# Expert results of a mixture-of-experts layer: block stores with an indexed gather, against an indexed scatter with plain loads

## What is computed

```python
# t: (512, 1024) normalised tokens; 4 groups x 8 experts, hidden width 512
g_sel  = argmax(t @ w_group + b_group)               # one group per token
e_logit = (t @ w_er[g_sel] + b_er[g_sel])            # 8 experts of that group
top_v, top_i = top_k(e_logit, 2)                     # two experts per token
gate   = softmax(top_v) * p_group
y[tok] = sum over its 2 experts e of gate * ((silu(t @ w_gate[e]) * (t @ w_up[e])) @ w_down[e])
x = x + y
```

## Time and profile before

| | |
|---|---|
| median of 3 runs | 1780.88 us (1779.61 to 1782.25) |
| profiled execution | 1782.86 us, span 1780.8 us |
| TensorE (PE) busy | 1412.7 us, 79% |
| VectorE (DVE) | 543.8 us, 31% |
| ScalarE (ACT) | 247.5 us, 14% |
| GpSimd (POOL) | 173.4 us, 10% |
| granted TensorE clock, mean | 0.906 of full speed |
| DMA | 486.05 MB, mean 273 GB/s |

### The profile page before, as it was taken

The page is one execution under the profiler, slowest core; times in us unless marked ns, Lnnn a source line. Parts: engine busy times, 40 slices in busy tenths (PEclk is TensorE's granted clock), DMA queues, the critical chain, the costliest instruction groups (busy, mean ns, idle before and its releaser), DMA issues. The chain is left out here.

```text
span 1780.8 us, 18695 instructions
## 1 busy us (share of the span) xinstructions
PE 1412.7 (79%) x7013; PEld 687.5 (39%) x7013; DVE 543.8 (31%) x1125; ACT 247.5 (14%) x501; POOL 173.4 (10%) x215
## 2 busy tenths in 40 slices
PE   6998756986988787878858978795998788788782
PEld 3444745542333333333313466653333233333330
DVE  6998598223101110110123156424011011011014
ACT  2201312110000000000001035410110000000001
POOL 0007160001000000000020000000110000000002
PEclk9999977987999999998987989996999899899896
DMA  7511403337999999999984200405899999999994
GB/s 233 157 56 25 38 13 145 151 145 281 390 406 404 408 417 411 409 408 407 412 333 164 95 1 1 177 37 227 325 399 408 406 411 406 404 409 410 407 417 169
DMA packets 75027, 486.05 MB, mean 273 GB/s; under 512 B 16752, under 2 KB 23536, under 8 KB 50016
## 3 DMA queue, kind: packets, MB, share of 16 engines
q1 hardware_dynamic: 53984, 440.26, 62.7%
q0 software_dynamic: 9472, 23.94, 4.3%
q10 hardware_dynamic: 11520, 21.15, 3.2%
HBM read 465.91 MB, written 27.79 MB: 277 GB/s over the span
## 5 line engine op out<-in xcount | busy, mean ns | idle before, releaser
L588 PE MATMUL psum<-ring,work 128*64 128x512 f32 x992 | 491.9, 654 | 133.6 <-DMA ring<-in_moe_w_up 130.7
L589 PE MATMUL psum<-ring,work 128*64 128x512 f32 x992 | 492.9, 655 | 0.0
L588 PEld LDWEIGHTS psum<-ring,work 128*64 128x64 f32 x992 | 144.3, 150 | 452.9 <-issue 449.4
L601 PE MATMUL psum<-ring,work 128*64 128x512 f32 x992 | 226.5, 598 | 31.2 <-DVE work L739 31.2
L736 DVE TENSOR_TENSOR work<-work,psum 64x512 f32<-64x512 f32 x64 | 44.1, 690 | 641.6 <-ACT work L693 599.3
L693 ACT ACTIVATE work<-psum 64x512 f32<-64x512 f32 x64 | 37.8, 591 | 842.1 <-PE psum L589 842.1
L589 PEld LDWEIGHTS psum<-ring,work 128*64 128x64 f32 x992 | 144.2, 150 | 0.0
L601 PEld LDWEIGHTS psum<-ring,work 128*64 128x64 f32 x992 | 66.6, 136 | 145.0 <-issue 125.2
L742 DVE COPY work<-psum 128x512 f32<-128x512 f32 x64 | 44.2, 691 | 247.7 <-PE psum L601 247.7
L1527 PE MATMUL psum<-ring,hT 128*128 128x512 f32 x256 | 112.1, 600 | 2.1 <-ACT work L1646 2.1
L883 POOL COPY ints<-ints 64x1 uint32 (+1 forms) x64 | 11.4, 179 | 818.7 <-PE psum L580 774.1
(11 more groups left out here) (350 smaller groups left out, 1425.8 us busy)
## 6 DMA issues: line engine op xcount, KB each, us to landing
ring<-in_moe_w_gate SPq DMA_DIRECT2D x62, 2048.0 KB
ring<-in_moe_w_up SPq DMA_DIRECT2D x62, 2048.0 KB, 23.2
ring<-in_moe_w_down SPq DMA_DIRECT2D x62, 2048.0 KB, 23.8
y_dram<-work ACTq DMA_DIRECT2D x128, 128.0 KB
ring<-in_hyb_w_in SPq DMA_DIRECT2D x5, 2048.0 KB, 9.7
ring<-in_swa_w_qkv SPq DMA_DIRECT2D x3, 2048.0 KB, 15.8
y_dram<-ones POOLq DMA_DIRECT2D x1, 4096.0 KB, 19.9
ring<-in_hyb_w_out SPq DMA_DIRECT2D x2, 2048.0 KB, 7.8
```

What stands on the lines that cost most here:

```text
L588: nc.tensor.matmul(bank[2 + b][0:BLK, :], XT[b][:, c, :], g[:, c, :], start=c == 0, stop=c == KC - 1)
L589: i = nc.tensor.matmul(bank[2 + b][BLK:P, :], XT[b][:, c, :], u[:, c, :], start=c == 0, stop=c == KC - 1)
L601: i = nc.tensor.matmul(bank[6 + b][BLK * hf:BLK * (hf + 1), :], HTE[b][:, c, :], d[:, c, hf * HALF:(hf + 1) * HALF], start=c == 0, stop=c ...
```

## The change

`y_dram` now has two rows of 2 KB (left and right half) for each assignment: row 2 * (512 k + token) + half. The router makes a second list: the one-hot block table is multiplied by 2 * (512 k + token) - 8192 and TensorE multiplies it twice with the place table, into the two halves of 128 partitions; with 8192 + half added (`SCL`) that is the target row of each partition of `YE`, and 8192 or more in an empty place. GpSimd issues, for each block, one indexed DMA that writes the 128 half rows of `YE` to their targets and skips those over 2047. In its loop GpSimd gathers the tokens of block e + 4 and then scatters the results of block e. ScalarE issues no stores. When all scatters have landed, SyncE reads the overflow count and issues eight plain loads of 512 KB for the combine, whose semaphores are now one for each tile. The calculation of `ROWI` and the fill at the start go.

```diff
-        y_dram = dram("y_dram", [NBLK * BLK, D])
+        y_dram = dram("y_dram", [2 * 2 * S, HALF])
...
+    put("srow", 2 * (np.arange(2 * NT)[None, :] * P + p[:, None]) - 2 * NOROW)
+    put("half", p[:, None] // BLK)
...
+            bs = shp(BL2, 8, NBLK)
+            pe.wait_ge(g_S.s, l + 1)
+            for hf in range(2):
+                for a in range(8):
+                    i = nc.tensor.matmul(bank[5][BLK * hf:BLK * (hf + 1), 0:NBLK], pl[:, a, :], bs[:, a, :], start=a == 0,
+                                         stop=a == 7)
+            i.then_inc(g_Sm.s, 1)
...
-            V(tv.tensor_tensor(bl, ins_dim(rt("ob"), 2, NBLK), ins_dim(cst("eid")[:, 0:NBLK], 1, 8), ALU.is_equal))
+            V(tv.tensor_tensor(bs, ins_dim(rt("ob"), 2, NBLK), ins_dim(cst("eid")[:, 0:NBLK], 1, 8), ALU.is_equal))
...
+            V.sync()
+            V(tv.tensor_tensor(bs, bs, ins_dim(cst("srow"), 2, NBLK), ALU.mult), g_S)
...
-            pi, a, b = rt("q").bitcast(I32), rt("qp").bitcast(I32), rt("ei").bitcast(I32)
-            V(tv.tensor_copy(pi, rt("pos")))
...
-            V(tv.tensor_copy(ROWI, rt("row")))
...
+            dve.wait_ge(g_Sm.s, l + 1)
+            V(tv.tensor_scalar(SCL, bank[5][:, 0:NBLK], cst("half"), 2.0 * NOROW, ALU.add, ALU.add), g_sc)
...
-            def store(e, par):
-                act.wait_ge(e_y, b0 + e + 1)
-                store_y1(act, par, e, y_st[par])
...
-                    dve.wait_ge(y_st[1 - par], 16 * b0 + (e - 3 - (1 - par)) * 16 + 32)
+                    dve.wait_ge(y_st[1 - par], 8 * b0 + (e - 3 - (1 - par)) * 8 + 16)
...
+            for t in range(NT):
+                for k in range(2):
+                    r0 = 2 * (S * k + P * t)
+                    sp.dma_start(YK[NT * k + t], y_dram[r0:r0 + 2 * P, :].rearrange("(p h) d -> p (h d)", h=2)).then_inc(
+                        yk_ld[t], 16)
...
+            def scatter_y(b, done):
+
+                pool.indirect_dma_start(y_dram, bass.IndirectOffsetOnAxis(SSTG[b], 0), YE[b], None, bounds_check=4 * S - 1,
+                                        oob_is_err=False).then_inc(done, 16)
+
+            def store(e, par):
+                pool.wait_ge(e_y, b0 + e + 1)
+                col = SCL[:, e:e + 1] if isinstance(e, int) else SCL[:, bass.ds(e, 1)]
+                pool.tensor_copy(SSTG[par], col).then_inc(e_sst, 1)
+                pool.wait_ge(e_sst, b0 + e + 1)
+                pool.sem_inc(pool_passed, 1)
+                scatter_y(par, y_st[par])
+
             fetch(0, 0)
             fetch(1, 1)
-            with pool.Fori(0, (NE - 2) // 2) as i:
+            fetch(2, 0)
+            fetch(3, 1)
+            pool.wait_ge(g_sc.s, l + 1)
+            with pool.Fori(0, (NE - 4) // 2) as i:
                 for k in range(2):
-                    fetch(i * 2 + 2 + k, k)
+                    fetch(i * 2 + 4 + k, k)
+                    store(i * 2 + k, k)
+            for e in range(NE - 4, NE):
+                store(e, e % 2)
...
-            for i in (k * NT + t for t in range(NT) for k in range(2)):
-                pool.indirect_dma_start(YK[i], None, y_dram, bass.IndirectOffsetOnAxis(ROWI[:, i:i + 1], 0)).then_inc(yk_ld[i], 16)
...
             for t in range(NT):
+                dve.wait_ge(yk_ld[t], 32 * (l + 1))
                 for k in range(2):
                     i = k * NT + t
-                    dve.wait_ge(yk_ld[i], 16 * (l + 1))
...
-            pool.dma_start(y_dram[NE * BLK:].rearrange("(p r) (c d) -> p (r c) d", p=P, d=P), ins_dim(ONES[:, :], 1, n)).then_inc(
-                fill_st, 16)
-            pool.wait_ge(fill_st, 16)
```

More of the change, by code:

```diff
@@ L64 @@
                   ("before", P), ("eye16", GC), ("gtie", NGRP), ("etie", EPG), ("eid", BLK), ("bidx", MAXOV + 1),
-                  ("tok", NT), ("place", BLK)]:
+                  ("tok", NT), ("place", BLK), ("srow", 2 * NT), ("half", 1)]:
     _COLS[_name] = (_N, _N + _w)
@@ L192, in encoder @@
             "consts_loaded", "x_loaded", "gain_loaded", "s5_rows_loaded", "s5_c_loaded", "s5_b_loaded", "router_loaded"))
-        fill_st = sem("y_rows_filled")
         pe_passed, pool_passed, sp_passed = (sem(n) for n in ("pe_wait_passed", "pool_wait_passed", "sp_wait_passed"))
@@ L347, in encoder @@
         INTS = sb("ints", 64 + NBLK + 2, U32)
-        ROWI = INTS[:, 0:8]
         PL1, BL1 = cut(WK, 11776, 8 * BLK), cut(WK, 12288, 8 * NBLK)
@@ L353, in encoder @@
         STG = [INTS[0:BLK, 64 + NBLK + b:65 + NBLK + b] for b in range(2)]
+        BL2 = cut(WK, 12288 + 8 * NBLK, 8 * NBLK)
+        SCL = rt("big")[:, 0:NBLK].bitcast(U32)
+        SSTG = [INTS[:, b:b + 1] for b in range(2)]
         assert 20 + MAXOV + 2 <= 64
@@ L362, in encoder @@
         g_L, g_Lm, g_sl = Count("router_places"), Count("router_lists_mm"), Count("router_lists")
+        g_S, g_Sm, g_sc = Count("router_targets"), Count("router_targets_mm"), Count("router_target_lists")
+        e_sst = sem("blk_targets")
         xg_ld = [sem(f"x_block{b}") for b in range(2)]
@@ L368, in encoder @@
         y_st = [sem(f"y_stored{b}") for b in range(2)]
-        yk_ld = [sem(f"y_rows{i}") for i in range(8)]
+        yk_ld = [sem(f"y_rows{t}") for t in range(NT)]
         ov = [{k: sem(f"ov{l}_{k}") for k in ("w", "i", "xg", "xt", "xe", "gu", "a", "h", "ht", "he", "dn", "y", "st")}
@@ L529, in dve_router @@
             V.sync()
-            bl = shp(BL1, 8, NBLK)
+            bl, bs = shp(BL1, 8, NBLK), shp(BL2, 8, NBLK)
             V(tv.tensor_tensor(shp(PL1, 8, BLK), ins_dim(rt("pos"), 2, BLK), ins_dim(cst("place"), 1, 8), ALU.is_equal))
-            V(tv.tensor_tensor(bl, ins_dim(rt("ob"), 2, NBLK), ins_dim(cst("eid")[:, 0:NBLK], 1, 8), ALU.is_equal))
+            V(tv.tensor_tensor(bs, ins_dim(rt("ob"), 2, NBLK), ins_dim(cst("eid")[:, 0:NBLK], 1, 8), ALU.is_equal))
             V.sync()
             for k in range(2):
-                V(tv.tensor_tensor(bl[:, NT * k:NT * (k + 1)], bl[:, NT * k:NT * (k + 1)], ins_dim(cst("tok"), 2, NBLK),
+                V(tv.tensor_tensor(bl[:, NT * k:NT * (k + 1)], bs[:, NT * k:NT * (k + 1)], ins_dim(cst("tok"), 2, NBLK),
                                    ALU.mult), g_L if k else None)
+            V.sync()
+            V(tv.tensor_tensor(bs, bs, ins_dim(cst("srow"), 2, NBLK), ALU.mult), g_S)
             V(tv.tensor_tensor(rt("cle").rearrange("p (b e) -> p b e", e=NE), ins_dim(rt("inc"), 1, MAXOV + 1),
@@ L720, in act_moe @@
                     xe(i * 2 + 2 + k, k)
-                    store(i * 2 + k, k)
                     silu(i * 2 + 2 + k, k)
-            for b in range(2):
-                store(NE - 2 + b, b)
             def body(j):
@@ L851, in sp_moe @@
             for b in range(2):
-                sp.wait_ge(y_st[b], 16 * NE * (l + 1))
+                sp.wait_ge(y_st[b], 8 * NE * (l + 1))
             def body(j):
@@ L859, in body @@
                     load_block_w(sp, ex + NE * l, 1, k, o["w"])
-                sp.wait_ge(o["y"], j + 1)
-                store_y1(sp, 1, j + NE, o["st"])
-                sp.wait_ge(o["st"], j * 32 + 32)
+                sp.wait_ge(o["st"], j * 16 + 16)
                 sp.sem_inc(sp_passed, 1)
             overflow_blocks(sp, l, body)
[L867 to L871, removed]
+            for t in range(NT):
[3 more added lines that the diff above has]
+                        yk_ld[t], 16)
         def pool_moe(pool, l, Q):
@@ L908, in body @@
                 pool.tensor_copy(STG[1], SLL[:, bass.ds(j + NE, 1)]).then_inc(o["i"], 1)
-                pool.wait_ge(o["i"], j + 1)
+                pool.wait_ge(o["i"], j * 2 + 1)
                 pool.sem_inc(pool_passed, 1)
                 gather_x(1, o["xg"])
-                pool.wait_ge(o["xt"], j + 1)
-            overflow_blocks(pool, l, body)
-            for b in range(2):
-                pool.wait_ge(y_st[b], 16 * NE * (l + 1))
-            overflow_wait(pool, l, "st", 32)
-            for i in (k * NT + t for t in range(NT) for k in range(2)):
-                pool.indirect_dma_start(YK[i], None, y_dram, bass.IndirectOffsetOnAxis(ROWI[:, i:i + 1], 0)).then_inc(yk_ld[i], 16)
[L922 to L926, removed]
+                pool.wait_ge(o["y"], j + 1)
+                pool.tensor_copy(SSTG[1], SCL[:, bass.ds(j + NE, 1)]).then_inc(o["i"], 1)
+                pool.wait_ge(o["i"], j * 2 + 2)
+                pool.sem_inc(pool_passed, 1)
+                scatter_y(1, o["st"])
+                pool.wait_ge(o["st"], j * 16 + 16)
+                pool.sem_inc(pool_passed, 1)
+            overflow_blocks(pool, l, body)
         def dve_combine(dve, l, V):
             for t in range(NT):
+                dve.wait_ge(yk_ld[t], 32 * (l + 1))
                 for k in range(2):
                     i = k * NT + t
-                    dve.wait_ge(yk_ld[i], 16 * (l + 1))
                     V(nc.vector.scalar_tensor_tensor(xv[:, t, :], YK[i], gates[:, i:i + 1], xv[:, t, :], ALU.mult,
@@ L2065, in _ @@
             pool.wait_ge(z_mm.s, 1)
```

(4 more changed lines are left out.)

## The result

| | before | after |
|---|---|---|
| median | 1781.06 us (7 runs, 1776.51 to 1784.21) | 1768.62 us (7 runs, 1764.55 to 1773.32) |
| ratio to before, 95% interval | | 0.9927 [0.9908, 0.9946] |
| profiled execution | 1782.86 us, span 1780.8 | 1765.54 us, span 1763.7 |
| first to last silu of the 32 experts, layer 0 / layer 1 | 478.87 / 479.00 us | 471.53 / 472.43 us |
| DMA | 486.05 MB | 473.48 MB |

The change saves 12.4 us, 0.7%. The forecast was a saving of 42 us, and the range ended at 1767: the time lies just above it, nearest to the rival "only the bytes count" (1763).

What follows compares the result with a forecast made beforehand. DMA engines were taken to pace the expert stages. 1782.9 - 41.8 (scatters) + 1.4 (router) - 1.5 (clock) + 0 = 1741.0, with the median 2.0 below the profiled run: 1739 us, range 1713 to 1767.

Steps and rivals of the forecast that it cites:

- only the bytes count: Rival: a result scatter saves only 0.31 us for its halved bytes, 18 us over 58 stores, so 1763 us; chance 0.20.
- What bounds the kernel: Expert stages: they run at the pace of the DMA engines (share 1.01), with TensorE having some 4 us room an expert.
- The price of a store: Expert stages: a store pair costs 1.44 us, from the rate's fall after its issue (1.47) and the stage's mean (1.43).
- Whichever the cost goes with, it halves: Scatter for two stores: half the bytes, pieces and DMAs, so 0.72 us saved on each of 58 stores, -41.8 us.
- the lower bound that the prediction had: Price of one result scatter if its bytes alone count: 0.131 MB / 430 = 0.31 us.
- the token gathers on that queue show no such fall here: Expert stages: token gathers on the software queue leave the rate at 430 GB/s; argued against software-made descriptors slowing two engines.
- Router, TensorE: Router: 16 added products take 3.9 us and delay layer 0's transposes by 1.4 us; zero in layer 1.
- Clock: TensorE at expert 0: added products fill idle gaps, so the higher clock may come earlier; -1.5 us for both layers together.
- Issue on GpSimd, ends of the layers, fill: Moving issue from ScalarE, the combine's start at each layer's end, and dropping the 4 MB fill: zero each.
- A scatter that costs more than two stores: Rival: a scatter holds the engines 2.2 us, 44 us more than now in all, so 1825 us; chance 0.07.
- empties that move bytes: Rival: the scatter's empty places move bytes after all and the cost stays, 1781 us; chance 0.07.
- As cheap as a gather: Rival: a scatter holds the engines only 0.31 us, like a gather, saving 66 us, so 1715 us; chance 0.14.

## Why the prediction was wrong, step by step

**What bounds the kernel: right.** DMA share 1.01 and TensorE's waits for weights stand in every variant looked at (1.00 in one), and each kernel's time follows the cost of its small transfers.

**The price of a store: wrong, and it carries the miss.** The step is "in the 6 us from the issue of a store pair at 506.86 it is 372", and "the same from the stage's mean". 1.44 us was the fall of the gather plus the store's bytes. Measured are 0.54 us (no stores), and 0.95 for the gather, which the prediction held free beyond its bytes. Their sum, 1.49 (1.61 with the gather by the rates), isn't far from the 1.75 of the prediction, 1.44 for the store and 0.31 for the gather as bytes: what the mean had to give was nearly right, the split was not. The step took the rate right after the gather's issue (430 in 500 to 506, issue at 503.14) for its effect, though its landing takes 8.8 us. Cut by the landing, the trace of before had the answer. The fall begins 4 us after the gather's issue, and a store pair of layer 1 issued at 1712.45, when no gather is under way any more (the last was issued at 1695.37), has none, though weights still stream:

```profile
507.00:511.50 4.50, 3.99 (x20) 1.72 (x22) 0.00 (x0) 0.00 (x0) 0.00 (x0) 1.00 1.00 347
1712.45:1718.45 6.00, 3.13 (x8) 1.14 (x10) 0.00 (x0) 0.00 (x0) 0.00 (x0) 0.73 0.99 421
```

**"Whichever the cost goes with, it halves": right in kind.** A store pair costs 0.54, a full scatter the same, and the skipped half saves 0.22. 0.54 - 0.22 = 0.32 us for a scatter is the lower bound that the prediction had (0.31). With 0.22 x 58 = 12.8 us saved and the rest of the prediction's sum the forecast would have been 1768. The saving is smaller than the rival's 18 us, since the stores cost less than their bytes at 430 GB/s. The rival "only the bytes count" was argued down by the earlier trace rows alone, which don't contradict it: the fall in them isn't the store's. For these writes over 128 partitions bytes alone come nearest; the cost beyond bytes was in another transfer. For the same reason "the token gathers on that queue show no such fall here" was a wrong reading: they show it, 4 us later.

**Router, TensorE: +1.4 was too much, +0.3 measured.** The new products take 3.23 us and not 3.9, and the transposes of layer 0 then started at once, where before they waited for the tokens. In layer 1 the transposes start 6.18 us after the first product (before: 6.17), so zero was right there.

**Clock: -1.5 forecast, about -0.8 in layer 0 and 0 in layer 1.** From the first list product to expert 0's silu it takes 17.50 us in layer 0 (18.03 before) and 17.86 in layer 1 (17.90). The granted clock rises from 1.2 to 2.4 GHz 12.1 us after that product in layer 0 where it was 13.4, and 13.2 us after it in layer 1 before and after. So the filled gaps may have gained a part of what was hoped for in one layer, and nothing in the other. Each of these is one execution and less than the scatter.

**Issue on GpSimd, ends of the layers, fill: zero, right.** VectorE waits for no scatter; the first two adds of the combine are done 0.16 us earlier than before (layer 1); the order of gather and scatter on the queue is worth nothing (1766.3 against 1768.6).

**The other rivals.** A scatter that costs more than two stores, and empties that move bytes, fell. "As cheap as a gather" had the scatter's price right, 0.32 us for its 0.31, but took the store's from the same 1.44 and so came to 1715.

**A slip that changes nothing.** With the bounds that the prediction states for the clock (0 to -2.8 us a layer) and the ends (-1 to +2 us a layer), its forecast runs from 1733 to 1745, not from 1735 to 1746.

## What to carry to other kernels

Where a kernel streams at the DMA limit, price a small transfer over the time until it lands, not from its issue, and look for a place in the trace where it stands alone before giving it a fall in rate. Two things that both happen once in a loop can't be told apart by the loop's mean. Give small loads beside such a stream 128 partitions (two blocks in one DMA): here that was worth three times what skipping half of the result writes was. And when a kernel lies between two others, look whether its cost is of the same kind before calling the differences parts of one sum.

## What the hardware showed unexpectedly

- A DMA of 64 places slows a stream of weights by more than its bytes: 0.95 us for 0.131 MB, against 0.24 when one DMA over 128 partitions brings two blocks. While it runs, a weight packet takes 0.80 us and not 0.61. The DMA share is 1.01 in both kernels; slower packets keep it full, and it shows nothing of the loss.
- A token gather beside the weights starts to cost only 4 us after its issue, and lands 8.7 us after it (median, in after; up to 10.3 in the other kernels with one block a gather). Scatters land after 8.0 to 8.6 us, in the six kernels whose profile gives it.
- Skipped places move no bytes on the queue (19.76 MB, against 28.14 with all places of the scatter filled, with 11248 packets in both), but the line on HBM counts them: it has 465.92 MB read in after, the same with all places of the gather filled, and 482.69 with 64 more empty places a block. These 16.8 MB didn't move on the queue (19.78 MB there). What the empty places cost by themselves, no run shows; the kernel with them is 20 us faster than after.
